# A DiT-like backbone on one core: the start rebuilt around VectorE sums, with the first step cut at four channel chunks

## The reference, cut to what matters

```python
def modulate(h, shift, scale): return h * (1 + scale) + shift
def swiglu(h, w_in, w_out):
    g, u = jnp.split(h @ w_in, 2, axis=-1)
    return (jax.nn.silu(g) * u) @ w_out
# DEPTH = 2 layers, SEQ = 512 tokens, D_MODEL = 1024, D_FF = 2816
m = jnp.split((silu(c) @ w_mod[i] + b_mod[i])[:, None, :], 9, axis=-1)   # 9 vectors of 1024
h = h + 0.5 * m[2] * swiglu(modulate(rms_norm(h), m[0], m[1]), w_ff_in[i, 0], w_ff_out[i, 0])
a = modulate(rms_norm(h), m[3], m[4]);  h = h + m[5] * mixer_i(a)         # layer 0 Fourier, layer 1 convolution
h = h + 0.5 * m[8] * swiglu(modulate(rms_norm(h), m[6], m[7]), w_ff_in[i, 1], w_ff_out[i, 1])
```

## Time and profile before

| what | value |
|---|---|
| time, median of 3 runs | 1848.27 us (1846.73 to 1848.34) |
| the profiled execution's own time | 1847.19 us |
| its span, first to last instruction | 1845.4 us |
| TensorE busy / granted clock over the span | 98% / 0.982 |
| VectorE, ScalarE, GpSimd busy | 65%, 33%, 9% |
| VectorE, TensorE and GpSimd instructions | 1539, 8656, 151 |
| the whole chain: TensorE's share | 86% |

### The profile page before, as it was taken

One profiled execution on the slowest core, in us unless ns is written; L12 is line 12 of the kernel. 1 busy time (PEld: TensorE's weight loads), 2 busy tenths in 40 slices (PEclk: granted clock), 3 DMA queues, 4 the chain that ended last, 5 costly groups with the idle time before them and its releaser, 6 DMA issues.

```text
span 1845.4 us, 22034 instructions
## 1 busy us (share of the span) xinstructions
PE 1800.1 (98%) x8656; PEld 1505.9 (82%) x8656; DVE 1195.4 (65%) x1539; ACT 602.5 (33%) x762; POOL 172.6 (9%) x151
## 2 busy tenths in 40 slices
PE   6999999998999999999999999999999999999999
PEld 6778888888898888888988888889765888888888
DVE  4776766767867676676776766547798555444454
ACT  1422222224343222222432222225677442222221
POOL 0000000002020000000200000002995200000000
PEclk6899999998999999999999999999999999999999
DMA  7664453531335445353254453421121322413201
GB/s 278 230 209 154 142 199 114 215 127 47 126 126 185 157 138 203 114 205 137 70 194 148 147 194 114 137 69 47 46 92 40 117 73 69 137 68 119 86 23 69
DMA packets 160395, 238.10 MB, mean 129 GB/s; under 512 B 3805, under 2 KB 110509, under 8 KB 160204
## 3 DMA queue, kind: packets, MB, share of 16 engines
q1 hardware_dynamic: 160016, 236.99, 37.0%
q10 hardware_dynamic: 316, 0.23, 0.0%
HBM read 235.11 MB, written 2.10 MB: 129 GB/s over the span
## 4 chain that ended last, share of the span: by engine, by line
PE 86%; DVE 4%; POOL 4%; ACT 3%; DMA 1%; issue 1%; SPq 0%; POOLq 0%; DVEq 0%; ACTq 0%
PE bank L1626 16%; PE bank L1633 16%; PE bank L1628 16%; PE bank L1505 10%; PE bank L1507 10%; PE bank L1506 10%; POOL tmp_c L626 3%; PE bank L1527 1%; PE bank L1859 1%; PE bank L1571 1%; PE bank L1573 1%; PE bank L1575 1%; DVE w_lo L968 1%; DMA raw_pair<-in_w_mod 1%; POOL sq_sum L591 1%
## 5 line engine op out<-in xcount | busy, mean ns | idle before, releaser
L1626 PE MATMUL bank<-a_hi,w_hi 128*128 128x512 f32 x1408 | 552.4, 392 | 3.4 <-ACT a_hi L677 1.9
L1628 PE MATMUL bank<-a_hi,w_lo 128*128 128x512 f32 x1408 | 549.3, 390 | 0.0
L1633 PE MATMUL bank<-a_lo,w_hi 128*128 128x512 f32 x1408 | 435.2, 390 | 1.5 <-DVE a_lo L1075 1.5
L1626 PEld LDWEIGHTS bank<-a_hi,w_hi 128*128 128x128 f32 x1408 | 265.2, 188 | 60.5 <-issue 3.4
L1633 PEld LDWEIGHTS bank<-a_lo,w_hi 128*128 128x128 f32 x1408 | 265.0, 188 | 57.8 <-DVE a_lo L1075 2.6
L1628 PEld LDWEIGHTS bank<-a_hi,w_lo 128*128 128x128 f32 x1408 | 265.3, 188 | 56.4 <-issue 1.4
L1193 DVE SCALAR_TENSOR_TENSOR h<-bank,half_gate,h 128x512 f32<-128x512 f32 x320 | 233.7, 748 | 109.8 <-PE bank L1507 109.2
L1505 PE MATMUL bank<-p_hi,w_hi 128*128 128x512 f32 (+1 forms) x768 | 286.6, 373 | 0.4 <-DVE h L1200 0.2
L1506 PE MATMUL bank<-p_hi,w_lo 128*128 128x512 f32 (+1 forms) x768 | 285.1, 371 | 0.0
L1507 PE MATMUL bank<-p_lo,w_hi 128*128 128x512 f32 (+1 forms) x768 | 285.1, 371 | 0.0
L968 DVE TENSOR_TENSOR w_lo<-raw_pair,w_hi 128x2048 fp32r<-128x2048 f32 x102 | 235.4, 2309 | 51.8 <-ACT w_hi L789 47.9
(11 more groups left out here) (191 smaller groups left out, 1843.0 us busy)
## 6 DMA issues: line engine op xcount, KB each, us to landing
raw_pair<-in_w_ff_in SPq DMA_DIRECT2D x88, 1024.0 KB, 7.1
raw_mod<-in_w_mod SPq DMA_DIRECT2D x66, 1024.0 KB, 8.4
raw_down<-in_w_ff_out SPq DMA_DIRECT2D x44, 1024.0 KB, 8.6
raw_pair<-in_conv_w_in SPq DMA_DIRECT2D x8, 1024.0 KB, 6.9
raw_pair<-in_w_mod SPq DMA_DIRECT2D x6, 1024.0 KB, 14.7
raw_pair<-in_fnet_w_out SPq DMA_DIRECT2D x4, 1024.0 KB, 6.4
raw_pair<-in_conv_w_out SPq DMA_DIRECT2D x4, 1024.0 KB, 6.6
raw_mod<-in_x SPq DMA_DIRECT2D x4, 512.0 KB, 4.9
```

What stands on the lines that cost most here:

```text
L1626: pe.matmul(ps[banks + s][:], tile_hi, a_hi[:, k], start=k == 0, stop=False, skip_group_check=True)
L1628: pe.matmul(ps[banks + s][:], tile_lo, a_hi[:, k], start=False, stop=False, skip_group_check=True)
L1633: ins = pe.matmul(ps[banks + s][:], w_hi[b][:, s * KD + k], a_lo[:, k], start=False, stop=k == KD - 1, skip_group_check=True)
```

## The change: what it does

The order of loads on SP is now x, unit 0, the first pair's channel chunks 0 to 3, unit 2, the first pair's chunks 4 to 7, without a wait between them; then, once all eight chunks are normed, units 1 and 3; then the second pair; then unit 4. The units have places of their own: two of them lie over buffers that are first used later (p_hi/p_lo and the third weight buffer).

Units 0 to 3 are now all summed on VectorE (`head_mac`), and TensorE adds over the partitions with 4 one-column matmuls per unit (`head_sum`); the last two channel chunks of unit 2 are done on TensorE directly (`head_direct`, 8 matmuls). There is no turn, fold or pick for them. First units 0 and 2 are made, which are shift and scale of channel chunks 0 to 3; units 1 and 3, for chunks 4 to 7, are made while TensorE works on the first four chunks. So step 0 runs over all four banks for chunks 0 to 3 (`chunk_rows`), with the two sums of units 1 and 3 ahead of and behind chunk 3, and then chunk by chunk for 4 to 7.

The squares of x are taken on the token rows with an accumulator, two by ScalarE and two by VectorE, and x is normed by TensorE itself: `head_normed` multiplies x rows by a diagonal of 1/rms, so that transposed and normed chunks come out in banks. GpSimd makes the low parts of the first pair, in four pieces of 128 x 1024. In step 1, unit 6 is summed after the first product instead of before it.

The diff, cut to its core:

```diff
+        VEC_BANK = 3
+        HEAD_BANKS = [3, 4]
+        LATE_BANK = [0, 1, 2, 0]
...
+            def first_pair(part, loaded):
+                w = up_weights(0)
+                dst = raw_pair[0][:].rearrange("p (s k) j n -> p s k (j n)", s=2)
+                rows = slice(4 * part, 4 * part + 4)
+                for s in range(2):
+                    sp.dma_start(dst[:, s, rows], w[:, rows, s * FF:s * FF + 2 * P]).then_inc(loaded, 16)
             head_load(0)
+            first_pair(0, s_first_in)
             head_load(2)
-            sp.wait_ge(s_h, KD)
+            first_pair(1, s_pair_in[0])
+            sp.wait_ge(s_head_n, KD)
+            head_load(1)
             head_load(3)
-            sp.wait_ge(s_mod_mac, KD)
-            head_load(1)
-            sp.wait_ge(s_head_sum, 1)
-            ff_pair(0, 0, 0)
-            sp.wait_ge(s_head_sum, 2)
+            sp.wait_ge(s_head_mac[0], KD)
+            ff_pair(0, 1, 1)
             for half, src in enumerate(mod_unit(0, HEAD * MU)):
+                sp.wait_ge(s_head_mac[1], 4 * (half + 1))
                 sp.dma_start(raw_mod[:, half], src).then_inc(s_mod_in[half], 16)
-            sp.wait_ge(s_mod_mac, 2 * KD)
-            ff_pair(0, 1, 1)
...
                 pool.tensor_copy(pick[lanes, P - QUAD:P], ident[lanes, lanes]).then_inc(s_pick, 1)
+            pool.wait_ge(s_pick, P // QUAD)
+            for part in range(2):
+                rows = slice(4 * part, 4 * part + 4)
+                for ch, (b, _) in enumerate(UP[0]):
+                    if part:
+                        pool.wait_ge(s_first, 2) if ch == 0 else pool.wait_ge(s_w[UP[0][0][0]], 1)
+                    elif ch:
+                        pool.wait_ge(s_first, 1)
+                    pool.wait_ge(s_w_hi[b], 1) if part else pool.wait_ge(s_first_hi, ch + 1)
+                    hi, lo = [w[b][:].rearrange("p (s k) n -> p s k n", s=2)[:, :, rows] for w in (w_hi, w_lo)]
+                    raw = raw_pair[0][:].rearrange("p (s k) j n -> p s k j n", s=2)[:, :, rows, ch]
+                    pool.tensor_tensor(lo, raw, hi.bitcast(F32), ALU.subtract).then_inc(
+                        s_w[b] if part else s_first, 1)
...
+            def head_modulated(ks):
+                act.wait_ge(s_mod, 2 if ks[0] < 4 else HEAD)
+                for k in ks:
+                    src = ps[4 + k][:] if k < 4 else normed_late[k - 4]
+                    act.activation(a_hi[:, k], src, ACT.Identity, bias=mod[:, 0, k:k + 1],
+                                   scale=mod[:, 0, KD + k:KD + k + 1]).then_inc(s_a_hi, 1)
+                    if k >= 2:
+                        act.wait_ge(s_a, k - 1)
+                    act.activation(tmp_c[:, k % 2], src, ACT.Identity, bias=mod[:, 0, k:k + 1],
+                                   scale=mod[:, 0, KD + k:KD + k + 1]).then_inc(s_a_full, 1)
+                    if k == 2 or k == 3:
+                        first_hi(1, k - 2)
...
+            act.wait_ge(s_row_sq[0], 2)
+            act.wait_ge(s_row_sq[1], 2)
+            act.activation(tok_std[:], tok_sq[:], ACT.Sqrt, bias=eps_col[:], scale=1.0 / D).then_inc(s_std, 1)
+            for d in range(4):
+                act.wait_ge(s_take, d + 1)
+                act.activation(h[:, d], ps[d][:], ACT.Copy).then_inc(s_h, 1)
+            for ch in range(2):
+                first_hi(0, ch)
+            for n in range(4):
+                act.wait_ge(s_head_n, 4 + n + 1)
+                act.activation(normed_late[n], ps[LATE_BANK[n]][:], ACT.Copy).then_inc(s_head_late, 1)
+            head_modulated(range(4))
+            head_modulated(range(4, KD))
             feed_forward(0, (FIRST[FNET][0], PAIR[FNET]))
...
+            def head_mac(g, n, ks):
+                unit = 2 * n + g
+                acc, rows = head_accs[n], head_rows[unit]
+                for k in ks:
+                    if k % 4 == 0:
+                        dve.wait_ge(s_head_in[2 * unit + k // 4], 16)
+                    if k == 0:
+                        if g > 0:
+                            dve.wait_ge(s_head_sum, n + 1)
+                        dve.tensor_scalar(acc[:], rows[:, k], silu_c[:, 0:1], None,
+                                          ALU.mult).then_inc(s_head_mac[g], 1)
+                    else:
+                        dve.wait_ge(s_head_mac[g], KD * n + k)
+                        dve.scalar_tensor_tensor(out=acc[:], in0=rows[:, k], scalar=silu_c[:, k:k + 1],
+                                                 in1=acc[:], op0=ALU.mult, op1=ALU.add).then_inc(s_head_mac[g], 1)
...
+            def head_lo(k):
+                dve.wait_ge(s_a_full, k + 1)
+                dve.tensor_tensor(a_lo[:, k], tmp_c[:, k % 2], a_hi[:, k].bitcast(F32),
+                                  ALU.subtract).then_inc(s_a, 1)
+            for k in range(4):
+                head_lo(k)
+                head_mac(1, 0, range(2 * k, 2 * k + 2))
+            head_mac(1, 1, range(KD))
+            head_columns(1)
+            for k in range(4, KD):
+                head_lo(k)
+                ring_mac(HEAD, range(2 * k - 8, 2 * k - 6))
             feed_forward(0, (FIRST[FNET][0], PAIR[FNET]))
...
-                    mod_turn(u0 - 1)
+                    gate_product(f, 0, 0)
+                    next_lo(f, 0, 0, 0)
+                    mod_turn(0)
+                    product_lo(f, 0, 0, 0)
+                    gated(f, 0, 1, 0)
+                    ring_mac(u0 + 1, range(4))
+                    next_lo(f, 0, 1, 0)
+                    mod_fold(0)
+                    ring_mac(u0 + 1, range(4, KD))
+                    mod_turn(1)
+                    mod_fold(1)
                 else:
...
+                    gated(f, i, 0, par)
+                    next_lo(f, i, 0, par)
+                    mod_mac(unit, mod_half_ready(16 * (FF_UNIT0[f] - HEAD + 3)), ring_rows)
+                    mod_turn(unit)
+                    gated(f, i, 1, par)
...
+            def head_direct(g, n):
+                unit = 2 * n + g
+                pe.wait_ge(s_head_in[2 * unit + 1], 16)
+                for j in range(UC):
+                    for k in range(KD - HEAD_DIRECT, KD):
+                        pe.matmul(ps[HEAD_BANKS[g]][:, n * UC + j:n * UC + j + 1], head_rows[unit][:, k, j * P:(j + 1) * P],
+                                  silu_c[:, k:k + 1], start=j == 0 and k == KD - HEAD_DIRECT, stop=False,
+                                  skip_group_check=True)
+            def head_sum(g, n, direct):
+                pe.wait_ge(s_head_mac[g], KD * n + KD - (HEAD_DIRECT if direct else 0))
+                for j in range(UC):
+                    ins = pe.matmul(ps[HEAD_BANKS[g]][:, n * UC + j:n * UC + j + 1],
+                                    head_accs[n][:, j * P:(j + 1) * P], ones[:, 0:1], start=j == 0 and not direct,
+                                    stop=True, skip_group_check=True)
...
+            def chunk_rows(b, banks, k, s_hi=None, s_lo=None):
+                if s_hi is not None:
+                    pe.wait_ge(s_hi, k + 1)
+                for bank in banks:
+                    tile_hi, tile_lo = w_hi[b[bank // 2]][:, bank % 2 * KD + k], w_lo[b[bank // 2]][:, bank % 2 * KD + k]
+                    pe.matmul(ps[bank][:], tile_hi, a_hi[:, k], start=k == 0, stop=False, skip_group_check=True)
+                    pe.matmul(ps[bank][:], tile_lo, a_hi[:, k], start=False, stop=False, skip_group_check=True)
+                if s_lo is not None:
+                    pe.wait_ge(s_lo, k + 1)
+                for bank in banks:
+                    ins = pe.matmul(ps[bank][:], w_hi[b[bank // 2]][:, bank % 2 * KD + k], a_lo[:, k], start=False,
+                                    stop=k == KD - 1, skip_group_check=True)
...
-                    up(f, 0, 1, False)
+                    b = [b for b, _ in UP[f]]
+                    pe.wait_ge(s_head_late, 4)
+                    pe.wait_ge(s_first, 2)
+                    for k in range(4):
+                        if k == 3:
+                            pe.wait_ge(s_a_full, 1)
+                            head_sum(1, 0, False)
+                        chunk_rows(b, range(4), k, s_a_hi, s_a)
+                    head_sum(1, 1, False)
+                    for ch in range(2):
+                        pe.wait_ge(s_w[b[ch]], UP[f][ch][1] + 1)
+                        for k in range(4, KD):
+                            ins = chunk_rows(b, [2 * ch, 2 * ch + 1], k, s_a_hi if ch == 0 else None,
+                                             s_a if ch == 0 else None)
...
+            def head_normed(k, bank):
                 for t in range(TC):
-                    ins = pe.transpose(ps[d % 4][:, t * P:(t + 1) * P], x_rows[:, t, d * P:(d + 1) * P], ident[:])
-                ins.then_inc(s_take, 1)
...
+                    ins = pe.matmul(bank[:, t * P:(t + 1) * P], x_rows[:, t, k * P:(k + 1) * P], head_diag[:, t],
+                                    start=True, stop=True, skip_group_check=True)
```

(46 more changed lines are left out.)

289 lines of the change are left out of this document (128 added, 161 removed).

## The result

The changed kernel takes 1832.09 us, the median of 4 runs (1829.95 to 1834.63), against 1847.59 (1846.73 to 1848.34) before: a ratio of 0.9918 with a 95% interval of 0.9903 to 0.9933, 15.5 us less. 1833.3 was predicted. The profiled execution took 1829.95 with a span of 1828.2, and is the fastest of the four.

A forecast was written before the change was run, and what follows sets the result against it. TensorE was taken to set the long-run pace, so only time before step 2 could change: 23.2 us gained at the first matmul, less 9.3 in step 0, plus 0.9 in step 1, called 15.0; 1833.3 us, range 1828.5 to 1838.5.

The forecast's parts named there:

- Term 1: Head, up to the first main matmul: starts at 36.5 us instead of 59.69, 23.2 us earlier; bounds 33.2 to 38.5.
- The disturbance: GpSimd's first two low-part pieces beside VectorE's sum of unit 2: cost 2.7 us, bounds nothing to 4.9.
- TensorE itself is not the bound here: Head: TensorE's transposes and products for normed x end by 30 us, under VectorE's sum.
- the lower bound of 33.2: Earliest start given for the first main matmul, if GpSimd does not disturb VectorE's sum of unit 2.
- Term 2: Step 0: takes 35.6 us instead of 26.27, giving back 9.3 us to waits for units 1 and 3.
- Term 3: Step 1 up to step 2's start: wait of 2.1 to 2.5 us before the pick, step 2 at 109.6.
- What shifts behind: From step 2 on: everything is TensorE's and shifts as it is, with later steps of 32.65 us.
- B: Head and step 0: GpSimd takes nothing from VectorE; gain 19 us, 1829.3 us; chance 0.26.
- C: Head and step 0: loads slower or lower clock lasts longer; gain 10 us, 1838.3 us; chance 0.19.
- D: Step 0: TensorE never leaves the lower clock, each wait dropping it again; 1852.8 us; chance 0.03.
- E: Half of step 0 runs at the lower clock or waits for units 1 and 3; gain 4, 1844 us; chance 0.05.

The follow-up runs named there:

- kernel with a filler in step 1: Changed kernel plus seven extra TensorE products, into a bank nobody reads, in the wait ahead of step 1's pick: 1830.84 us, ratio 0.9907 to the kernel before.
- kernel with unit 6 first: Changed kernel with unit 6's sum moved back ahead of the gate's first product in step 1: 1831.76 us, ratio 0.9909 to the kernel before.
- the cut undone: Changed kernel with units 1 and 3 also summed ahead of the first main matmul, which waits for all four units: 1836.11 us, ratio 0.9934 to the kernel before.

## Why the prediction was right

- **Term 1, the first matmul at 36.5:** measured 36.52, with each step near its place. Unit 0 landed at 20.5 (20.6 said), unit 2's second half at 28.6 (28.85), the sum ended at 33.3 (33.4), GpSimd's pieces ran at 24.70 to 29.54 (24.6 to 29.5). The disturbance took 2.7 us of VectorE as assumed; since that was a pick between 0 and 4.9, to meet it to the tenth is luck. The six products are 0.49 + 3.97 alone (as the kernel with the low parts on VectorE shows), and 1.24 + 5.93 here. One claim beside this term was wrong: "TensorE itself is not the bound here" left out the eight direct products of unit 2 and the sums of unit 0. Without GpSimd's reads VectorE is done at 30.4 to 30.6, but TensorE only at 34.2 to 34.4, and the first matmul comes at 35.5 to 35.7, only about 1 us earlier. So the lower bound of 33.2 (33.8 by the term's own numbers) could not be reached.
- **Term 2, step 0 at 35.6 us:** measured 34.5. Unit 1's sum was ready at 49.4 (49.9), GpSimd's last two pieces having cost 4.3 us (4.0), and unit 3's at 55.4 (55.9). The way from unit 3's sum to a_hi of chunk 4, for which I took 2.5 us "as in term 1", was 1.4 (55.4 to 56.84), since TensorE's clock was full there and the four sums took 1.05 instead of 1.87. That belongs to this execution. In the kernel with a filler in step 1, which has the same program up to there, these sums ran at the lower clock:

```profile
55.67 1.76 PE L1632 MATMUL bank<-ones,mod_turned 128*128 128x1 f32 x8 [2.03 <-DVE mod_turned L1429]
58.69 0.76 PE L1722 MATMUL bank<-a_hi,w_hi 128*128 128x512 f32 x1 [1.26 <-ACT a_hi L714]
```

There the way is 2.1 us and step 0 takes 35.3; in the kernel with unit 6 first it is 2.3 and 35.5, and step 2 starts at 109.48, where 109.6 was said. Chunks 4 to 7 went at VectorE's pace, one in 2.05 us (2.3 said). The recorded terms for them add up to 67.6; that 66.7 was taken instead has no reason there, and it was the better number. The loads of units 1 and 3 ended no wait.
- **Term 3, step 1:** the wait ahead of the pick was 2.04 (2.1 to 2.5 said), and the clock fell behind it as before. Step 1 took 37.48 us, 37.5 said (72.1 to 109.6). Here too the terms gave 85.5 for the pick and 85.1 was carried without a reason.
- **What shifts behind:** 15.8 us at step 2, and 17.2 us in the two profiled spans. The rest arose behind the first SwiGLU, in the norm. There the clock fell in both traces, but at different work: it was 0.50 from 437 to 450 us before; after, it was 0.50 from 417 to 419 and 0.62 from 425 to 430. These 1.4 us belong to the execution and not to the change: from step 2 to the end it is 1721.0 us before, 1719.7 in the changed kernel, and 1721.0 and 1720.9 in the two kernels with the filler and with unit 6 first, whose program behind step 2 does the same work.
- **The rivals.** B (GpSimd takes nothing) is settled against: without its reads 5.1 to 5.4 us are won up to step 2, and 7.6 to 7.8 in the medians. That is more than the 4 assumed for its absence, and less than the 9.9 us that the four pieces run. The Trainium skill's rule ("SBUF — State Buffer", section "Who interferes with whom") says that a VectorE instruction with two SBUF inputs and a GpSimd instruction that reads SBUF exclude each other for a whole instruction; the rows of 2.89 and 3.67 us agree, each with some 2.15 us more. But the rule gives the price of a collision, not of the stage: of the 2.7 us lost in unit 2's sum only about 1 reached the first matmul, with TensorE late next. C and D (a clock that stays low) did not come: in the profiled execution it was low four times in steps 0 and 1 (windows above) and came back each time within some 4 us of work. It can last longer: 7 us behind the pick in the kernel with the taps in two DMAs. E was wrong too, though its mechanism is the largest single one: with the cut undone one sees that 9.9 of 13.9 us are given back.

## What to carry to other kernels

When work is moved out of the way of the first matmul, add up what VectorE must still do before the next fixed point: here the start came 23.2 us earlier and step 0 gave 8.3 back, to waits for the same sums, to their TensorE part and to the lower clock behind the waits. Compare starts with a second execution before reading 1 us into them, and look at the whole time too: two gains that add up to step 2 need not be seen adding at the end. Before giving an idle GpSimd a helper's job, ask what VectorE reads in that moment; the same four pieces were cheaper in VectorE's own waits. Look at the landing time of each early load against its neighbours, because one small transfer of 31 rows held up the early large loads of the head, in both kernels, and two lines cured it.
